# Two runs of 256 columns for one of 512: the moving side of the input and up projections of a hybrid decoder step

## The reference

```python
h = rms_norm(x, g_mix_pre)
z = h @ w_in                                  # 1024 -> 2048
y_a = pool_mixer(z[..., :gw], ...)            # four mixers of width 256
y_b = conformer_conv(z[..., gw:3 * gw], ...)
y_c = chunk_spatial_gating(z[..., 3 * gw:5 * gw], ...)
y_d = short_gated_conv(z[..., 5 * gw:], ...)
o = jnp.concatenate([y_a, y_b, y_c, y_d], axis=-1) @ w_out   # 1024 -> 1024
x = x + rms_norm(o, g_mix_post)
f = rms_norm(x, g_ffn_pre)
f = jnp.square(jax.nn.relu(f @ w_up)) @ w_down                # 1024 -> 4096 -> 1024
x = x + rms_norm(f, g_ffn_post)
```

## Time and profile before

| | |
|---|---|
| median of 3 runs | 2289.42 us (2289.16 to 2293.85) |
| profiled execution, its own time | 2289.91 us |
| its span, first to last instruction | 2288.1 us |
| mean granted TensorE clock | 0.977 of full |
| PE busy | 2147.0 us (94%), 14425 matmuls |
| weight loads busy | 1945.0 us (85%) |
| DVE busy | 1081.4 us (47%) |
| ACT busy | 752.6 us (33%) |

### The profile page before, as it was taken

How to read it: one execution, slowest core, us unless ns; L and a number is a source line. 1 busy time by engine, 2 the same in 40 slices (tenths; PEclk the granted TensorE clock), 3 DMA queues, 4 the chain that set the end, 5 groups by cost and what they waited for, 6 DMA issues and landing times.

```text
span 2288.1 us, 32980 instructions
## 1 busy us (share of the span) xinstructions
PE 2147.0 (94%) x14425; PEld 1945.0 (85%) x14425; DVE 1081.4 (47%) x1388; ACT 752.6 (33%) x1145; POOL 115.0 (5%) x205
## 2 busy tenths in 40 slices
PE   6989997979699999999999999999999989999996
PEld 4877775768488988988898899889898989999996
DVE  3677766775643333465333346533334553334243
ACT  4233232224333223443323244332324442313131
POOL 2000110010000000000000000000000000000000
PEclk9999998989799999999999999999999999999998
DMA  6754644553232223445233334533223434222221
GB/s 211 242 212 170 212 169 170 180 192 103 102 112 93 93 93 102 131 154 166 93 99 99 98 130 148 166 100 102 93 93 119 137 115 135 85 83 78 90 74 60
DMA packets 186084, 291.87 MB, mean 128 GB/s; under 512 B 6128, under 2 KB 162453, under 8 KB 177733
## 3 DMA queue, kind: packets, MB, share of 16 engines
q1 hardware_dynamic: 160997, 168.64, 23.2%
q0 software_dynamic: 24656, 120.96, 15.0%
q10 hardware_dynamic: 287, 0.16, 0.0%
HBM read 247.24 MB, written 42.80 MB: 127 GB/s over the span
## 4 chain that ended last, share of the span: by engine, by line
PE 66%; issue 18%; DVE 7%; ACT 4%; DMA 3%; ACTq 0%; POOL 0%; SPq 0%; POOLq 0%; DVEq 0%
PE mm L1695 21%; PE mm L1696 21%; PE mm L1697 21%; ACT w_hi L635 2%; DVE w_lo L1079 2%; DVE conv L1122 2%; DMA mixc<-mixT_scratch 1%; DMA x_in<-in_x_prompt 1%; PE tr L1700 1%; PE tr L1729 1%; DMA raw<-in_w_in 1%; PE tr L1921 0%; DVE o_sb L1399 0%; PE mm L1756 0%; DVE conv_s L1606 0%
## 5 line engine op out<-in xcount | busy, mean ns | idle before, releaser
L1079 DVE TENSOR_TENSOR w_lo<-raw,w_hi 128x2048 fp32r<-128x2048 f32 x152 | 348.4, 2292 | 707.1 <-ACT w_hi L635 707.1
L1695 PE MATMUL mm<-act_hi,w_hi 128*128 128x512 f32 (+1 forms) x1728 | 638.5, 369 | 9.8 <-DVE act_lo L1417 6.0
L1696 PE MATMUL mm<-act_lo,w_hi 128*128 128x512 f32 (+1 forms) x1728 | 632.6, 366 | 0.0
L1697 PE MATMUL mm<-act_hi,w_lo 128*128 128x512 f32 (+1 forms) x1728 | 630.0, 365 | 0.0
L1695 PE MATMUL mm<-w_hi,u_hi 128*128 128x256 f32 (+1 forms) x2176 | 603.3, 277 | 1.5
L1697 PE MATMUL mm<-w_hi,u_lo 128*128 128x256 f32 (+1 forms) x2176 | 601.0, 276 | 0.0
L1696 PE MATMUL mm<-w_lo,u_hi 128*128 128x256 f32 (+1 forms) x2176 | 600.9, 276 | 0.0
L635 ACT ACTIVATE w_hi<-raw 128x2048 fp32r<-128x2048 f32 x152 | 290.8, 1913 | 582.0 <-PE mm L1697 581.1
L1695 PEld LDWEIGHTS mm<-w_hi,u_hi 128*128 128x128 f32 (+1 forms) x2176 | 398.3, 183 | 4.8 <-DVE u_lo L1433 3.6
L1696 PEld LDWEIGHTS mm<-w_lo,u_hi 128*128 128x128 f32 (+1 forms) x2176 | 398.3, 183 | 1.2
L1697 PEld LDWEIGHTS mm<-w_hi,u_lo 128*128 128x128 f32 (+1 forms) x2176 | 398.3, 183 | 0.7
(11 more groups left out here) (238 smaller groups left out, 1350.4 us busy)
## 6 DMA issues: line engine op xcount, KB each, us to landing
raw<-in_w_ffn_up SPq DMA_DIRECT2D x64, 1024.0 KB, 5.4
raw<-in_w_ffn_down SPq DMA_DIRECT2D x64, 1024.0 KB, 5.1
w_hi<-whi_scratch POOLq DMA_DIRECT2D x24, 1024.0 KB, 5.2
w_lo<-wlo_scratch POOLq DMA_DIRECT2D x24, 1024.0 KB, 7.9
raw<-in_w_out SPq DMA_DIRECT2D x16, 1024.0 KB, 5.3
raw<-in_w_in SPq DMA_DIRECT2D x8, 1024.0 KB, 9.5
whi_scratch<-w_hi POOLq DMA_DIRECT2D x8, 1024.0 KB, 8.7
wlo_scratch<-w_lo POOLq DMA_DIRECT2D x8, 1024.0 KB, 10.7
```

The source lines that it names most:

```text
L1079: DVE.tensor_tensor(w_lo[:, s, :, :], raw[:, s, :, :], w_hi[:, s, :, :].bitcast(fp32), ALU.subtract)\
L1695: PE.matmul(out, whi, xhi, start=(k == 0), stop=False)
L1696: PE.matmul(out, whi, xlo, start=False, stop=False)
L1697: return PE.matmul(out, wlo, xhi, start=False, stop=(k == K - 1))
```

## The change

In the I panels with moving tokens and in the U panels, a bank of exactly 512 moving tokens is filled by two passes over the eight slices, columns 0 to 255 first and then 256 to 511, where it was filled by one pass with 512 columns. Runs of 272 (block 3), VV, the samples, O and D are not touched. The semaphore increment stays on the last matmul of the bank.

```diff
+            def pieces(c0, c1):
+
+                return [(c0, c0 + PC), (c0 + PC, c1)] if c1 - c0 == 2 * PC else [(c0, c1)]
...
                             c = slice(t * P, (t + 1) * P)
-                            for k in range(K):
-                                last_mm = three(bank[:, :], w_hi[:, s, k, c], w_lo[:, s, k, c],
-                                                act_hi[:, k, 0:N1], act_lo[:, k, 0:N1], k)
+                            for c0, c1 in pieces(0, N1):
+                                for k in range(K):
+                                    last_mm = three(bank[:, c0:c1], w_hi[:, s, k, c], w_lo[:, s, k, c],
+                                                    act_hi[:, k, c0:c1], act_lo[:, k, c0:c1], k)
                             last_mm.then_inc(tile_done, 1)
...
                             bank = take_bank(j, i)
-                            for k in range(K):
-                                last_mm = three(mm[bank][:, 0:c1 - c0], w_hi[:, s, k, c], w_lo[:, s, k, c],
-                                                act_hi[:, k, c0:c1], act_lo[:, k, c0:c1], k)
+                            for a0, a1 in pieces(c0, c1):
+                                for k in range(K):
+                                    last_mm = three(mm[bank][:, a0 - c0:a1 - c0], w_hi[:, s, k, c], w_lo[:, s, k, c],
+                                                    act_hi[:, k, a0:a1], act_lo[:, k, a0:a1], k)
                             last_mm.then_inc(bank_done[bank], 1)
```

## The result

The changed kernel is slower: 2309.96 us median (2308.51 to 2313.92, 4 runs) beside 2290.74 us before (4 runs), a ratio of 1.0085 with a 95% interval of 1.0067 to 1.0103. The sign and PE's pace as the main cause were forecast; the size was 19 us where 13 were said (0.85% where 0.57% stood). The time lies above the likeliest case (2298 to 2309 us) and at the very edge of the whole range (2285 to 2310 us). The profiled execution took 2308.51 us, its span 2306.8 us, 18.7 us more than before.

A forecast was written before the change was run, and what follows sets the result against it. The prediction took PE's pace to bound the kernel. Profiled 2289.91 + 13.2 for the pairs - 0.1 for half-clock stretches = 2303.0 us, less 0.5 to the median: 2302.5 us (+0.57%), range 2285 to 2310 us.

The forecast's parts named there:

- the likeliest case: Whole kernel: the time comes to 2298 to 2309 us; the slower outcome, 2295 to 2310 us, had chance 0.52.
- What bounds the kernel: PE, busy 94% of the span with 66% of the chain, bounds the whole kernel; its pace reaches the end.
- the long wait of the I stage: PE's wait before the transposes at 386.78: its chain starts from PE's own bank, so a later PE delays it too.
- The price of a pair: I and U panels: two 256-column matmuls take 237.0 ns, 3.6 ns over one of 512; 3648 pairs give 13.2 us.
- No wait moves: PE's waits: bank taking, increment and the reader's work per bank stay as they were, so no wait changes.
- That the weight loads hide, since D would show it if they did not,: I and U panels: doubled loads hide behind moving columns, since D sustains one load per 113.4 ns; no cost.
- The first rival: I and U pairs: surplus goes with the columns, a pair costs what one matmul cost; 2290.5 us, chance 0.34.
- The second rival: I and U pairs: 512 columns have their own surplus, pairs run at D's pace; -24.3 us, 2265 us, chance 0.14.
- The figure of the Trainium skill: I and U panels: about 2.5 ns fixed per matmul at the full clock, 3648 times, an estimate of 9 us.

The follow-up runs named there:

- u_only: The changed kernel with the I panels as before, so only the U panels run in halves; 2302.80 us, 1.0049 of before.
- act64: The kernel before with act_hi and act_lo allocated right behind w_lo, act distance 0 instead of 96; 2286.11 us, 0.9978 of before.
- act64_u32: act64 with u_hi and u_lo also shifted by a pad, u distance 96 instead of 64; 2305.34 us in one run, beside 2290.65 of before.
- act_m32: The kernel before with act_hi and act_lo allocated behind eps and v_small, act distance 32; 2295.86 us, 1.0018 of before.
- act_m64: The kernel before with act_hi and act_lo allocated behind cst, act distance 64; 2276.20 us, 0.9927 of before.
- all_m64: The kernel before with w and act tiles all behind cst, distance 0 for act and u; 2315.11 us, 1.0106 of before.
- narrow: The kernel before with the 32-sample-token bank in block 3's O and D panels filled by two 128-column runs; 2291.90 us beside 2293.72.
- after64: The changed kernel with act_hi and act_lo allocated right behind w_lo, act distance 0; 2313.38 us, 1.0102 of before.
- after_m64: The changed kernel with act_hi and act_lo allocated behind cst, act distance 64; 2290.68 us, 0.9994 of before.
- unequal: The changed kernel with 512 columns cut into 384 + 128 in I and 320 + 192 in U; 2420.70 us, one run.
- quarters: The changed kernel with the 512 columns in four runs of 128 instead of two of 256; 3273.33 us, one run.

## Why the prediction was right in sign and wrong in size

**What bounds the kernel** held: PE's pace reached the end. The span grew by 18.7 us, 16.1 of them 3648 pairs at the measured 4.4 ns; u_only is in proportion. That the long wait of the I stage moves along with PE and absorbs nothing was right: 14.0 us before, 14.2 after. The two further long waits of PE before the first U panel, which the prediction doesn't name, are unchanged at 14.9 and 15.6 us. Two terms of the sum failed.

**The price of a pair** was mis-sized: 3.6 ns from the straight line through 272 and 512 columns, 4.4 ns measured, 16 us in place of 13.2. The line took its 272 columns as rows of "the same tiles". They are, but every second run lies at another distance, so that 125.69 ns is the mean of 126.3 and 125.1. With the runs that lie where the 512 columns lie (126.3) the same line gives 5.1 ns a pair, 18.6 us, too much. That the prediction came within a quarter of the price is thus partly luck: no straight line holds. The runs of 320 and 384 show a fixed part of about 1.9 ns a matmul, and 256 and 272 columns lie some 1.3 ns above their line. Of the 4.4 ns a pair, about 1.9 is the second fixed part and 2.6 is twice that rise. This split is read off the widths at distance 96. What the rise is stays open. That the columns come near the 111.7 ns of the load would fit, but in D and O 256 columns behind a quarter of the load are no faster at distances 64 and 96, and U has no rows with a smaller load.

**"No wait moves"**, costed at nothing, is the other: 2.6 us around the O panels of block 3. The stretch from PE's first O matmul of block 3 to its first D matmul behind it, with the wait of PE inside it and the DMA `mixc<-mixT_scratch` ahead of that wait, in the profiles of all thirteen kernels:

| kernels | DMA, us | PE stands, us | granted clock | stretch, us |
|---|---|---|---|---|
| I and U whole: before, act64, act64_u32, act_m32, act_m64, all_m64, narrow | 5.22 to 5.45 | 0.77 to 1.51 | 1.00 | 56.2 to 57.9 |
| only U split: u_only | 5.89 | 1.92 | 1.00 | 58.3 |
| I and U split: after, after64, after_m64, unequal, quarters | 6.22 to 6.67 | 1.93 to 2.73 | 0.97 | 59.0 to 60.6 |

The groups do not overlap, so this wait does belong to the change, though each kernel has only one profile. Why a DMA in block 3 takes longer when the I and U panels are split, no run tells.

**That the weight loads hide, since D would show it if they did not,** was wrong as an argument. D lies at distance 64, where 128 stationary columns cost no more than 32 even with 256 moving ones; at distance 0 D itself does show it, 118.8 against 114.3 ns. So D could not speak for panels that lie at another distance. Below 256 columns loads do not hide at all (111.7 ns for 192 and 128).

**The first rival**, that the surplus goes with the columns, rested on the twofold O and VV pitch equalling the 512-column one. That was an accident of the layout: O and VV went to 118.9, 118.3 and 113.3 ns and 512 columns to 232.2, 234.5 and 230.0 when the act tiles were moved, and twice the one is no longer the other. **The second rival**, D's pace, took D's 113.4 ns for a property of the width; it is a property of a distance of 64 bytes between the tiles. At that distance the 256-column runs of U reach 116.7 ns, not 113.3.

**The figure of the Trainium skill** ("TensorE: Matmul & The Clock Gate", section "Wait — 56ns, not 53.3ns?"), 2.5 ns a matmul, by which the price came to 9 us, is near the 1.9 ns fixed part of the runs of 320 to 512 columns. It has neither the floor nor the dependence on the distance.

## What to carry to other kernels

Keep the moving side at the full bank where it can be had. Cutting a run of 512 columns in two cost 3.4 to 5.6 ns a pair here, according to where the tiles lay, and pieces of 192 or 128 columns are paced by the stationary operand (111.7 ns for 128 columns of it), whatever they stream. Read the pitch from start to start, since the busy time of overlapping matmuls hides it, and don't compare pitches of stages, or of runs within one stage, whose tiles lie differently. In a kernel bound by fp32 matmuls the place of the operand tiles is worth a try: moving two allocations from a distance of 96 bytes to one of 64 (modulo 128) gave 0.73% here, nearly as much as the change lost.

## What the runs showed of the hardware that was not expected

- The pitch depends on the distance between the stationary and the moving tile modulo 128 bytes: for 512 moving columns 232.2, 234.5, 230.0 and 233.3 ns at 0, 32, 64 and 96; for 256 moving weight columns behind 128 columns of act or u 118.9, 118.3, 113.3 and 116.7 ns. Why, no run tells. Nor do the runs say why 256 columns have 116.7 ns in U and 113.3 ns in D at the same distance of 64.
- In quarters the granted clock stayed at its lower level (1.2 GHz, 0.50) for long stretches in which PE was busy without a pause. It had fallen in the waits ahead of the first U panel, as it does in before (31 us with PE busy for 7.8 of them). In before it is back within 3 us of the first U matmul; in quarters it was not back in 162 us of 128-column matmuls, and came back some 3 us into the 256-column matmuls of the D panel behind them. Later the same 128-column matmuls ran at the full clock. The windows (us, PE busy, granted clock, DMA share, GB/s) of the waits, of the U panels, of the D panel and of a later U stretch:

```profile
984.50:1015.70 31.20, 7.79 (x32) 0.50 0.42 152
1016.00:1178.00 162.00, 162.00 (x766) 0.50 0.06 21
1186.00:1200.00 14.00, 14.00 (x125) 1.00 0.51 153
1360.00:1440.00 80.00, 80.00 (x719) 1.00 0.17 54
```

  At the half clock that is 212 ns a matmul, 1.9 times the 111.6 of the full clock, so the floor runs with the clock. The mean granted clock of the execution is 0.912 where the changed kernel has 0.976. Quarters took 963 us more than the changed kernel, where the floor alone gives 3648 x (4 x 111.7 - 237.8) = 762 us; the lower clock is worth about (0.976 - 0.912) x 3272 = 209 us by an estimate, which is the rest.
- The timeline's duration of a 128-column matmul behind 128 stationary columns (0.28 us in quarters) is that of a 256-column one; behind 32 it is 0.22 us.
